# Hybrid decoder layer on one core: the mixing stage's last third in a new order, the exponent's argument split between GpSimd and ScalarE

## The chip, the cores and the metric

One core of a Trainium2 chip. The metric is the device time of one execution in microseconds, median of several runs. Engines: TensorE (PE, its weight loads PEld), VectorE (DVE), ScalarE (ACT), GpSimd (POOL) and SyncE (SP, which here only starts DMA transfers). A queue's name with a q (SPq, ACTq) stands for what that engine issues.

## The reference, cut to what matters

A layer with three groups of heads on one normed input (1024 prompt tokens, 8 sample tokens, width 1024), then an MLP. The part that the change touches is the mLSTM group (4 heads of 96, chunks of 128 tokens) and, in its order, the pooling group:

```python
bcum = jnp.cumsum(lfb, axis=-1)
D = bcum[..., :, None] - bcum[..., None, :] + ib[..., None, :]
D = jnp.where(mask, D, -jnp.inf)
m_t = jnp.maximum(g, jnp.max(D, axis=-1))
S = jnp.einsum('bhtd,bhsd->bhts', qb, kb) * jnp.exp(D - m_t[..., None])
num = jnp.einsum('bhts,bhsd->bhtd', S, vb) + inter[..., None] * jnp.einsum('bhvk,bhtk->bhtv', C, qb)
...
s = cg[:, PBUF+1:PBUF+1+L] - cg[:, PBUF+1-win:PBUF+1-win+L]     # pooling: windows 2, 4, 8, 16
diff = s / cnt[None, :, None] - u
outs.append(jnp.einsum('blc,cd->bld', diff, pool_w[gi]) * pool_scale[gi])
```

## The kernel before, in words

The whole layer runs feature-major in fp32. Each dense product is made of three matmuls for each of 8 row tiles (high part by high, low by high, high by low, lines 2407 to 2409), so 24 matmuls of 344 tokens for one output tile and one of the three token ranges. The high part of a tile or weight is a ScalarE copy into fp32r (lines 1234, 1239), the low part a GpSimd subtraction (w_lo, line 1082; lo, line 1087).

**The order of work** of the mixing stage is written out by hand in MIX_ORDER (lines 92 to 171). Every engine walks the same list and does its own share of each word, in that order, so a word's place sets its place in the queue of each engine. The words of the stretch:

- D:u:c, dense product of unit u and token range c. ScalarE empties its bank (D0, D1, D2). For units 14 to 16 it applies a gelu (line 1331), VectorE multiplies by the LRU result (line 1870), then come the high and low parts, which are pieces of Y.
- W:u, split of the weights of unit u. W_hi has two cells, so ScalarE waits for the last product of unit u-2; GpSimd follows with W_lo. Unit 17 is the first of the output projection, which starts the stage after this one.
- ADA, ADT, ADM: modulation products on TensorE, their turn (line 2392), and the addition on VectorE (line 1717). R:n: ScalarE issues the DMA of raw weights n.
- LD:c: SyncE loads K, Q, V and NM of mLSTM chunk c. NM (minus m_t over the tokens, broadcast to 128 partitions, 256 KB) has one buffer; the load waits on SyncE for the semaphore of the previous chunk (line 884). From chunk 2 on, LD also waits for U:c-2 and B:c-2.
- EX:c: VectorE adds COL's column and NM into EX (line 1885), takes the minimum with MASK (line 1886), and ScalarE takes the exponent in place (line 1368). S:c: TensorE turns K into the bank X3 (line 2498, KT:c) and multiplies K by Q (line 2502, bank X0). SX:c: VectorE scales K into KW (line 1892, frees X3) and multiplies EX by S (line 1895).
- AB:c: Q by state (line 2514, B, bank X2) and EX by V (line 2520, A, bank X1). NU:c: VectorE scales B into T1 (line 1900) and adds A into NUM (line 1903), which frees both banks. HN:c (lines 1907 to 1914, then a square root on ScalarE, line 1371) and HM:c (lines 1918, 1919) norm the result; U:c and CN:c (lines 2528, 1923, 1925) bring the state forward.
- Y:c: TensorE turns the result (line 2536, bank X3); YD:c: VectorE multiplies it by the gate (line 1936, three instructions) and frees X3, then high and low parts; SyncE loads the next gate (load_o).
- POOLV:j, the window sums of pooling tile j: tile 0 on GpSimd, tile 1 on VectorE (lines 1949 to 1953 and ten instructions of lines 1060 to 1065). POOLS copies half of them on ScalarE, POOLD takes the difference (tile 0 on GpSimd, line 1135; tile 1 on VectorE, line 1965). POOL:j:c multiplies by the pooling weights (line 2549) into X1 for c 0 and 2, X2 for c 1; POOLY:j:c reads the bank twice on ScalarE (lines 1392, 1393), and GpSimd makes the low part.

So POOL:0:0 needs X1 from NU:6, and POOL:1:c needs POOLD:1. The X banks are handed out in the order of the list, each use waits for the one before it to be freed (take, line 2362). ScalarE loads another table (ACT_TABLE_LOAD) when it changes between exponent, square root and gelu.

Of the kernel before, what the change touches and what calls it, by code (L numbers as in the profile page):

```python
# [17 lines left out]
ALU = mybir.AluOpType  # L18
# [6 lines left out]
D = 1024  # L25
# [10 lines left out]
HEADS, HD = 4, 96  # L36
# [51 lines left out]
def unit_of(kind, t):  # L88
# [109 lines left out]
def bank_uses(plan):  # L198
# [8 lines left out]
    for s in plan:  # L207
# [7 lines left out]
        elif k == "ADT":  # L215
            add(s, "X1" if s[1] in ADA_START else "X4" if s[1] == NPAIR - 1 else "X3")
# [73 lines left out]
def build(nc, I, O):  # L290
# [24 lines left out]
    with ExitStack() as ctx:  # L315
# [197 lines left out]
        ex_ready, ex_exp, cn_ready = sem("ex_ready"), sem("ex_exp"), sem("cn_ready")  # L513
# [284 lines left out]
        def _(sp):  # L798
# [26 lines left out]
            for s in plan:  # L825
# [41 lines left out]
                elif k == "LD":  # L867
# [15 lines left out]
                    if c >= 1:  # L883
                        sp.wait_ge(ex_ready, c)
# [193 lines left out]
        def _(pool):  # L1078
# [25 lines left out]
            for s in plan:  # L1104
# [108 lines left out]
        def _(act):  # L1213
# [55 lines left out]
            for s in plan:  # L1269
# [407 lines left out]
        def _(dve):  # L1677
# [78 lines left out]
            for s in plan:  # L1756
# [1129 lines left out]
```

## Time and profile before

| | |
|---|---|
| three runs, median | 1175.29 us (1174.09 to 1179.2) |
| the profiled execution | 1175.78 us, span 1174.0 us |
| busy in the span | PE 1124.6 us (96%), DVE 792.8 (68%), ACT 473.4 (40%), POOL 346.9 (30%) |
| granted TensorE clock, mean | 0.982 |
| changed stretch | from about 228 us (first loads of mLSTM chunk 0) to 383.5 us (first output product) |

Busy time is time in which an engine executes something. TensorE's matmuls overlap; its idle time is read from the waits, where each row says which instruction stood still and whose result it waited for. The granted clock is given as a share of 2.4 GHz; 0.5 is 1.2 GHz. The share of one engine in the whole span says little here: the stages differ, and in the MLP, from about 500 us on, TensorE has no idle time at all.

### The profile page before, as it was taken

Reading aid. Unit: us, or ns where it says so; the run is one execution under the profiler, and the core shown is the slowest. Engines: PE = TensorE matmul, PEld = TensorE weight load, DVE = VectorE, ACT = ScalarE, POOL = GpSimd, SP = SyncE. Lnnn points to the kernel's source line nnn. Section 1 sums busy time; section 2 is a strip of 40 time slices with the busy share of each in tenths; the row PEclk is TensorE's granted clock in tenths of the full one; section 3 lists DMA queues with packets and bytes.
Section 4 is the critical chain, followed back from the end, with each engine's and each line's share of the span. In section 5 each row is a group of like instructions: output and inputs, shape, how many; then the busy total and the mean of one; then the engine's idle time right before and its main releaser. Section 6 shows DMA issues by size and latency. Waiting matters only on the chain.

```text
span 1174.0 us, 19681 instructions
## 1 busy us (share of the span) xinstructions
PE 1124.6 (96%) x7237; PEld 1077.3 (92%) x7237; DVE 792.8 (68%) x1319; ACT 473.4 (40%) x780; POOL 346.9 (30%) x275
## 2 busy tenths in 40 slices
PE   4799999999989999999999999999999999999997
PEld 1598888888979999899999999999999999999996
DVE  4561455478775434678578878778778788788546
ACT  5551355655456344642233332332432433433431
POOL 0442011201434357764032022132131231231352
PEclk9699999998989999999999999999999999999998
DMA  8912523566523722111111111202102202111104
GB/s 302 326 57 88 142 90 126 177 180 218 176 87 113 269 90 73 54 55 37 37 36 55 54 37 55 71 18 71 56 16 75 68 18 72 53 50 58 37 1 145
DMA packets 67846, 109.85 MB, mean 94 GB/s; under 512 B 6435, under 2 KB 42567, under 8 KB 67399
## 3 DMA queue, kind: packets, MB, share of 16 engines
q1 hardware_dynamic: 57574, 84.88, 22.0%
q10 hardware_dynamic: 10208, 24.12, 6.6%
q8 instruction: 41, 0.67, 0.2%
q14 instruction: 23, 0.18, 0.0%
HBM read 96.81 MB, written 12.18 MB: 93 GB/s over the span
## 4 chain that ended last, share of the span: by engine, by line
PE 82%; DVE 9%; ACT 3%; DMA 2%; issue 1%; POOL 1%; SPq 1%; ACTq 0%; POOLq 0%; DVEq 0%
PE D L2407 7%; PE D L2409 7%; PE D L2408 7%; PE D L2591 6%; PE D L2593 5%; PE D L2592 5%; PE X L2593 5%; PE X L2591 5%; PE X L2592 5%; PE X L2663 5%; PE X L2664 5%; PE X L2665 5%; PE D L2663 2%; PE D L2665 2%; PE D L2664 2%; DMA RAWW<-in_WADA 2%
## 5 line engine op out<-in xcount | busy, mean ns | idle before, releaser
L2407 PE MATMUL D<-H_hi,W_hi 128*128 128x344 f32 x472 | 158.6, 336 | 3.7 <-POOL H_lo L1087 3.1
L2409 PE MATMUL D<-H_hi,W_lo 128*128 128x344 f32 x472 | 152.4, 323 | 0.0
L2408 PE MATMUL D<-H_lo,W_hi 128*128 128x344 f32 x472 | 152.4, 323 | 0.0
L1087 POOL TENSOR_TENSOR Y_lo<-FU,Y_hi 128x344 fp32r<-128x344 f32 (+3 forms) x84 | 100.1, 1194 | 154.2 <-ACT Y_hi L1521 88.5
L1082 POOL TENSOR_TENSOR W_lo<-RAWW,W_hi 128x1024 fp32r<-128x1024 f32 x25 | 61.6, 2465 | 182.5 <-ACT W_hi L1234 182.2
L1087 POOL TENSOR_TENSOR Y_lo<-EY,Y_hi 128x344 fp32r<-128x344 f32 (+1 forms) x24 | 38.3, 1598 | 216.3 <-ACT Y_hi L1521 144.5
L2407 PEld LDWEIGHTS D<-H_hi,W_hi 128*128 128x128 f32 x472 | 90.5, 192 | 11.8 <-issue 7.6
L2408 PEld LDWEIGHTS D<-H_lo,W_hi 128*128 128x128 f32 x472 | 90.3, 191 | 0.9 <-issue 0.5
L2409 PEld LDWEIGHTS D<-H_hi,W_lo 128*128 128x128 f32 x472 | 90.2, 191 | 0.0
L2215 DVE SCALAR_TENSOR_TENSOR X<-X,MOD 128x344 f32<-128x344 f32 (+1 forms) x138 | 75.7, 566 | 9.2 <-PE X L2665 9.0
L2663 PE MATMUL X<-Y_hi,W_hi 128*128 128x344 f32 x252 | 80.7, 320 | 0.0
L2664 PE MATMUL X<-Y_lo,W_hi 128*128 128x344 f32 x252 | 80.6, 320 | 0.0
L2665 PE MATMUL X<-Y_hi,W_lo 128*128 128x344 f32 x252 | 80.5, 319 | 0.0
L2017 DVE SCALAR_TENSOR_TENSOR X<-D,MOD,X 128x344 f32<-128x344 f32 (+1 forms) x72 | 41.3, 573 | 45.4 <-PE D L2593 24.7
L2407 PE MATMUL D<-Y_hi,W_hi 128*128 128x344 f32 x192 | 62.0, 323 | 1.5 <-POOL W_lo L1082 1.5
L1099 POOL TENSOR_TENSOR SS<-SS,SQ 128x344 f32<-128x344 f32 x45 | 43.3, 963 | 65.9 <-ACT SQ L1430 40.5
L1087 POOL TENSOR_TENSOR Y_lo<-KEPT,Y_hi 128x344 fp32r<-128x344 f32 x24 | 26.4, 1098 | 120.7 <-ACT Y_hi L1521 120.7
L2408 PE MATMUL D<-Y_lo,W_hi 128*128 128x344 f32 x192 | 61.3, 319 | 0.0
L2409 PE MATMUL D<-Y_hi,W_lo 128*128 128x344 f32 x192 | 61.3, 319 | 0.0
L1556 ACT ACTIVATE W_hi<-RAWW 128x1024 fp32r<-128x1024 f32 x30 | 31.8, 1059 | 64.3 <-PE X L2665 55.6
L2378 PE MATMUL X<-RAWW,CTX 128*32 128x256 f32 x384 | 35.7, 461 | 19.5 <-DMA RAWW<-in_WADA 19.4
L1087 POOL TENSOR_TENSOR H_lo<-FU,H_hi 128x344 fp32r<-128x344 f32 (+2 forms) x33 | 29.9, 914 | 66.2 <-ACT FU L1252 50.7
(416 smaller groups left out, 3455.1 us busy)
## 6 DMA issues: line engine op xcount, KB each, us to landing
RAWW<-in_W SPq DMA_DIRECT2D x76, 512.0 KB, 3.6
RAWW<-in_WADA ACTq DMA_DIRECT2D x28, 512.0 KB, 4.1
RAWW<-in_WADA SPq DMA_DIRECT2D x20, 512.0 KB, 8.0
RAWW<-in_W ACTq DMA_DIRECT2D x18, 512.0 KB, 3.7
X0T<-in_x SPq DMA_DIRECT2D x3, 1376.0 KB, 12.8
out_y<-OUTN SPq DMA_DIRECT2D x24, 172.0 KB
X<-in_x SPq DMA_DIRECT2D x8, 344.0 KB, 5.3
NM<-nm_d SPq DMA_DIRECT2D x8, 256.0 KB, 5.3
```

What stands on the lines that cost most here:

```text
L1082: nc.gpsimd.tensor_tensor(lo_v, RAWW[:, raw, :] if src is None else src[:], hi_v.bitcast(F32), ALU.subtract).then_inc(w_lo_ready, 1)
L1087: nc.gpsimd.tensor_tensor(lo_v, fu_v, hi_v.bitcast(F32), ALU.subtract).then_inc(lo_ready, 1)
L2215: V.scalar_tensor_tensor(out=X[:, m, c * CH:c * CH + w], in0=ps[:, 0:w], scalar=MOD[:, 5 * KT + m, 0:1], in1=X[:, m, c * CH:c * CH + w], o ...
L2407: T.matmul(out, w_h, hi[:, kt, a:b], start=(kt == 0), stop=False)
L2408: T.matmul(out, w_h, lo[:, kt, a:b], start=False, stop=False)
L2409: one = T.matmul(out, w_l, hi[:, kt, a:b], start=False, stop=(kt == KT - 1))
L2591: T.matmul(out, w_h, hi(kt), start=(kt == 0 and not onto), stop=False, skip_group_check=onto)
L2592: T.matmul(out, w_h, lo(kt), start=False, stop=False, skip_group_check=onto)
L2593: one = T.matmul(out, w_l, hi(kt), start=False, stop=(kt == n - 1), skip_group_check=onto)
L2663: T.matmul(bank[:, 0:CH], w_hi[:, a:a + P], h, start=(start and k == 0), stop=False, skip_group_check=onto)
L2664: T.matmul(bank[:, 0:CH], w_hi[:, a:a + P], l, start=False, stop=False, skip_group_check=onto)
L2665: one = T.matmul(bank[:, 0:CH], w_lo[:, a:a + P], h, start=False, stop=(stop and k == 1), skip_group_check=onto)
```

## The change

The exponent: GpSimd adds MASK to NM in place (new word NX:c, one instruction of 128x512) as soon as NM has landed. ScalarE takes the exponent straight from NM into EX with COL's column as bias, one instruction per head (four of 128x128) in place of one of 128x512. VectorE's two instructions go, and with the minimum goes the cap of the exponent's argument at 0. ScalarE now waits for A:c-1 before it writes EX. NM is loaded again after the exponent, no longer after VectorE's addition.

The order: NX:c+1 stands after NU:c (NX:6 after ADM:21, NX:7 before EX:7). YD:0 stands ahead of HN:4. W:15 moves behind NU:5 and HN:5; ADM:21 and EX:6 move ahead of HM:5. NU:6, Y:3, POOL:0:0 and POOL:0:1 with their POOLY stand before POOLV:1; HN:6, LD:7 and HM:6 move into D:15:0; R:60 moves to D:14:0; W:17 moves from D:16:1 to D:15:2. ADT:22 writes bank X4 in place of X3.

```diff
--- before.py
+++ after.py
@@ -144,29 +144,28 @@
 D:8:1 R:43
 D:8:2 R:42 ADA:16:1 R:44 W:10 LD:0 SMA TS TSD ADT:16 LRUM:2
 D:9:0
-D:9:1 R:46 R:45 LD:1 ADM:16 EX:0 ADA:17:0 S:0 SX:0 ADA:17:1 W:11 AB:0 R:47
-D:9:2 ADT:17 U:0 NU:0 HN:0 CN:0 ADM:17 HM:0 EX:1 ADA:18:0 SMK S:1 SX:1 SMB:0
+D:9:1 R:46 R:45 LD:1 ADM:16 NX:0 EX:0 ADA:17:0 S:0 SX:0 ADA:17:1 W:11 AB:0 R:47
+D:9:2 ADT:17 U:0 NU:0 NX:1 HN:0 CN:0 ADM:17 HM:0 EX:1 ADA:18:0 SMK S:1 SX:1 SMB:0
 D:10:0 LD:2
-D:10:1 LD:3 AB:1 NU:1 ADA:18:1 U:1 CN:1 HN:1
+D:10:1 LD:3 AB:1 NU:1 NX:2 ADA:18:1 U:1 CN:1 HN:1
 D:10:2 HM:1 R:49 R:48 LD:4 EX:2 W:12
-D:11:0 SMB:1 S:2 SX:2 AB:2 NU:2 ADT:18 U:2 CN:2 ADM:18 HN:2 R:50
+D:11:0 SMB:1 S:2 SX:2 AB:2 NU:2 NX:3 ADT:18 U:2 CN:2 ADM:18 HN:2 R:50
 D:11:1 SMB:2 HM:2 R:52 EX:3 ADA:19:0 S:3 SX:3
-D:11:2 SMB:3 AB:3 ADA:19:1 W:13 LDO:0 R:51 NU:3
+D:11:2 SMB:3 AB:3 ADA:19:1 W:13 LDO:0 R:51 NU:3 NX:4
 D:12:0 ADT:19 U:3 HN:3 HM:3 R:53 CN:3 ADM:19 LD:5 ADA:20:0 EX:4 R:55
-D:12:1 S:4 SX:4 ADA:20:1 Y:0 R:54 SMC AB:4 NU:4
-D:12:2 R:56 U:4 ADT:20 HN:4 W:14 YD:0 R:58 HM:4 LD:6
+D:12:1 S:4 SX:4 ADA:20:1 Y:0 R:54 SMC AB:4 NU:4 NX:5
+D:12:2 R:56 U:4 ADT:20 YD:0 HN:4 W:14 R:58 HM:4 LD:6
 D:13:0 Y:1 ADM:20 CN:4 ADA:21:0 EX:5 YD:1 R:57
-D:13:1 S:5 ADA:21:1 POOLV:0 YS POOLS:0 POOLD:0 SX:5 W:15 YSD AB:5 NU:5 HN:5 HM:5
-D:13:2 ADT:21 R:59 U:5 CN:5
-D:14:0 Y:2 ADM:21 EX:6 YD:2
-D:14:1 ADA:22:0 S:6 SX:6 R:61 AB:6 ADA:22:1 Y:3 POOLV:1
-D:14:2 POOL:0:0 POOLS:1 NU:6 YD:3 R:60 POOLY:0:0 POOL:0:1 ADT:22 POOLY:0:1 HN:6 LD:7 POOL:0:2 POOLD:1 POOLY:0:2 ADM:22
-    HM:6
-D:15:0 U:6 Y:4 POOL:1:0 R:62 CN:6 POOLY:1:0 ADA:23:0 EX:7 POOL:1:1 W:16 R:64 YD:4
+D:13:1 S:5 ADA:21:1 POOLV:0 YS POOLS:0 POOLD:0 SX:5 YSD AB:5 NU:5 HN:5 W:15
+D:13:2 ADT:21 ADM:21 NX:6 EX:6 HM:5 R:59 U:5 CN:5
+D:14:0 R:60 Y:2 YD:2
+D:14:1 ADA:22:0 S:6 SX:6 R:61 AB:6 NU:6 ADA:22:1 Y:3 POOL:0:0 POOLY:0:0 POOL:0:1 POOLY:0:1 POOLV:1
+D:14:2 POOL:0:2 ADT:22 POOLS:1 POOLY:0:2 YD:3 POOLD:1 ADM:22
+D:15:0 HN:6 LD:7 U:6 HM:6 POOL:1:0 Y:4 R:62 CN:6 POOLY:1:0 ADA:23:0 NX:7 EX:7 POOL:1:1 W:16 R:64 YD:4
 D:15:1 POOLY:1:1 S:7 SX:7 POOL:1:2 POOLY:1:2 ADA:23:1 R:63
-D:15:2 Y:5 YD:5 AB:7 NU:7 ADT:23 HN:7
-D:16:0 R:65 HM:7 Y:6 U:7 YD:6 CN:7 ADM:23
-D:16:1 Y:7 W:17 YD:7
+D:15:2 W:17 Y:5 YD:5 AB:7 NU:7 ADT:23 HN:7
+D:16:0 R:65 Y:6 YD:6 HM:7 U:7 CN:7 ADM:23
+D:16:1 Y:7 YD:7
 D:16:2
 """
 
@@ -213,7 +212,7 @@
         elif k == "ADA" and s[2] == 0:
             add(("ADA", s[1]), "X3" if s[1] in ADA_START[::2] else "X4")
         elif k == "ADT":
-            add(s, "X1" if s[1] in ADA_START else "X4" if s[1] == NPAIR - 1 else "X3")
+            add(s, "X1" if s[1] in ADA_START else "X4" if s[1] >= NPAIR - 2 else "X3")
         elif k in ("G1", "G2", "G3", "G4", "Y", "YS"):
             add(s, "X3")
         elif k == "TS":
@@ -510,7 +509,7 @@
         ts_stored, u_diff = sem("ts_stored"), [sem(f"u{j}_diff") for j in range(POOL_T)]
         ld_kqv = [sem(f"ld_kqv{b}") for b in range(2)]
         ld_nm, ld_o, ld_mask = sem("ld_nm"), sem("ld_o"), sem("ld_mask")
-        ex_ready, ex_exp, cn_ready = sem("ex_ready"), sem("ex_exp"), sem("cn_ready")
+        nm_masked, ex_exp, cn_ready = sem("nm_masked"), sem("ex_exp"), sem("cn_ready")
         z_ready, z_root, hm_ready = sem("z_ready"), sem("z_root"), sem("hm_ready")
         sma_t, sma_e, sr_stored = sem("sma_t"), sem("sma_e"), sem("sr_stored")
         ld_st, ld_s, ld_bdl = sem("ld_state"), sem("ld_s"), sem("ld_bdl")
@@ -881,7 +880,7 @@
                         sp.dma_start(dst[:], src.rearrange("(h d) t -> d h t", d=HD)[:, :, c * LC:(c + 1) * LC]).then_inc(ld_kqv[b], 16)
                     sp.dma_start(VB[b][:].rearrange("p h v -> p (h v)"), v_d[c]).then_inc(ld_kqv[b], 16)
                     if c >= 1:
-                        sp.wait_ge(ex_ready, c)
+                        sp.wait_ge(ex_exp, c)
                     sp.dma_start(NM[:], nm_d.rearrange("(h c) t -> c h t", c=NLC + 1)[c].partition_broadcast(P)).then_inc(ld_nm, 16)
                 elif k == "SMA":
                     sp.wait_ge(sma_e, 2)
@@ -1121,6 +1120,11 @@
                 elif k == "POOLY":
                     key = ("POOL", *s[1:])
                     lo(full_at[key], *views(key))
+                elif k == "NX":
+                    if s[1] == 0:
+                        pool.wait_ge(ld_mask, 16)
+                    pool.wait_ge(ld_nm, 16 * (s[1] + 1))
+                    nc.gpsimd.tensor_tensor(NM[:], NM[:], over(MASK[:], HEADS), ALU.add).then_inc(nm_masked, 1)
                 elif s == ("POOLV", 0):
 
                     pool.wait_ge(h_ready, LRU_T)
@@ -1364,8 +1368,16 @@
                     act.wait_ge(gv, 4)
                     nc.scalar.activation(GR[:, R_EM, :], GR[:, R_EM, :], ACT.Exp, scale=-1.0).then_inc(ga, 1)
                 elif k == "EX":
-                    act.wait_ge(ex_ready, s[1] + 1)
-                    nc.scalar.activation(EX[:], EX[:], ACT.Exp).then_inc(ex_exp, 1)
+                    c = s[1]
+                    if c == 0:
+                        b, n = use[("G4",)]
+                        act.wait_ge(x_free[b], n + 1)
+                    else:
+                        wait_full(act, ("A", c - 1))
+                    act.wait_ge(nm_masked, c + 1)
+                    for h in range(HEADS):
+                        one = nc.scalar.activation(EX[:, h, :], NM[:, h, :], ACT.Exp, bias=colh(0, c)[:, h:h + 1])
+                    one.then_inc(ex_exp, 1)
                 elif k == "HN":
                     act.wait_ge(z_ready, s[1] + 1)
                     nc.scalar.activation(SM4[:, 5, :], SM4[:, 4, :], ACT.Sqrt, bias=EPT[:], scale=1.0 / HD).then_inc(z_root, 1)
@@ -1874,16 +1886,9 @@
                         wait_full(dve, ("TS", w))
                         put_free(V.tensor_copy(QK8[:, w, :], bank(("TS", w))[0:DEC, 0:HEADS * HD]), ("TS", w))
                 elif k == "EX":
-                    c = s[1]
-                    if c == 0:
+                    if s[1] == 0:
                         tell(V.memset(CN[:], 0.0), cn_ready, 1)
                         dve.wait_ge(ld_dec, 16)
-                        dve.wait_ge(ld_mask, 16)
-                    else:
-                        wait_full(dve, ("A", c - 1))
-                    dve.wait_ge(ld_nm, 16 * (c + 1))
-                    link(V.tensor_tensor(EX[:], NM[:], wide(colh(0, c), LC), ALU.add))
-                    tell(V.tensor_tensor(EX[:], EX[:], over(MASK[:], HEADS), ALU.min), ex_ready, c + 1)
                 elif k == "SX":
                     c = s[1]
                     if c:
```

## Rows read from the trace of the kernel before

**Rows 1.** The profile page, first line.

```profile
span 1174.0 us, 19681 instructions
```

**Rows 2.** Busy by stretch: length, PE, PEld, DVE, ACT, POOL (instructions), clock, DMA, GB/s.

```profile
700.00:800.00 100.00, 100.00 (x637) 100.00 (x636) 81.83 (x132) 35.24 (x54) 23.78 (x17) 1.00 0.15 48
```

**Rows 3.** Waits from 225 to 400 us: in total, times, longest.

```profile
PE X L2549 <- DVE NUM L1903: 3.7, 1, 3.7
...
PE X L2520 <- DVE EX L1895: 2.9, 3, 1.7
...
PE D L2407 <- POOL W_lo L1082: 1.5, 1, 1.5
...
PE X L2536 <- DVE MOD L1717: 1.5, 1, 1.5
...
PE X L2392 <- DVEq L1941: 0.9, 1, 0.9
```

**Rows 4.** Busy by stretch, columns as in rows 2.

```profile
230.00:240.00 10.00, 8.99 (x73) 7.67 (x72) 6.80 (x18) 2.64 (x4) 0.00 (x0) 1.00 0.86 256
266.00:278.00 12.00, 10.33 (x59) 9.55 (x58) 9.48 (x19) 5.29 (x7) 2.34 (x1) 0.72 0.59 199
344.00:354.00 10.00, 9.24 (x40) 7.85 (x41) 7.57 (x15) 7.38 (x12) 5.20 (x5) 0.68 0.61 158
```

**Rows 5.** The tile EX: count, ns min/median/max, first and last start.

```profile
L1886 DVE TENSOR_TENSOR EX<-EX,MASK x8: 691/693/1302, 234.0 to 356.9; 128x512 f32<-128x512 f32 x8
L1368 ACT ACTIVATE EX<-EX x8: 629/632/635, 235.3 to 358.3; 128x512 f32<-128x512 f32 x8
```

**Rows 6.** Line 1363, a ScalarE instruction with a bias from memory.

```profile
L1363 ACT ACTIVATE GR<-GR x1: 387/387/387, 134.7 to 134.7; 36x128 f32<-36x128 f32 x1
```

**Rows 7.** ScalarE in order of time: start us, duration us.

```profile
346.37 0.55 ACT L1392 ACTIVATE Y_hi<-X,COLS 128x344 fp32r<-128x344 f32 x1
346.81 0.54 ACT L1393 ACTIVATE FU<-X,COLS 128x344 f32<-128x344 f32 x1
...
358.27 0.64 ACT L1368 ACTIVATE EX<-EX 128x512 f32<-128x512 f32 x1 [0.51 <-DVE EX L1886]
...
358.81 1.04 ACT L1234 ACTIVATE W_hi<-RAWW 128x1024 fp32r<-128x1024 f32 x1
...
360.28 1.28 ACT L1331 ACT_TABLE_LOAD   x1
```

**Rows 8.** GpSimd by line and form, 310 to 385 us: busy us, mean ns.

```profile
L1087 POOL TENSOR_TENSOR Y_lo<-FU,Y_hi 128x344 fp32r<-128x344 f32 x15 | 14.9, 995 | 26.5 <-ACT Y_hi L1239 25.0 <-ACT FU L1393 1.4
...
L1082 POOL TENSOR_TENSOR W_lo<-RAWW,W_hi 128x1024 fp32r<-128x1024 f32 x3 | 7.1, 2376 | 2.3 <-ACT W_hi L1234 2.2
```

**Rows 9.** The tile NM, time of its eight loads.

```profile
DMA to landing us min/median/max: 3.2/5.3/7.2
```

**Rows 10.** GpSimd in order of time.

```profile
286.67 2.40 POOL L1082 TENSOR_TENSOR W_lo<-RAWW,W_hi 128x1024 fp32r<-128x1024 f32 x1 [18.02 <-ACT W_hi L1234]
```

**Rows 11.** VectorE in order of time.

```profile
286.86 2.62 DVE L1912 TENSOR_TENSOR HM<-NUM,SM 128x384 f32<-128x384 f32 x1
...
335.05 0.19 DVE L1949 COPY UO<-ST 128x15 f32<-128x15 f32 x1
...
344.65 1.12 DVE L1936 SCALAR_TENSOR_TENSOR FU<-X,COLS,OT 128x128 f32<-128x128 f32 x3
...
349.63 1.29 DVE L1965 SCALAR_TENSOR_TENSOR ST<-PB,COLS,ST 128x1024 f32<-128x1024 f32 x1
...
362.88 0.56 DVE L1892 TENSOR_TENSOR KW<-X,COL 128x384 f32<-128x384 f32 x1 [0.21 <-DVEq L1969]
```

**Rows 12.** TensorE in order of time.

```profile
366.62 0.49 PE L2536 MATMUL X<-IDN,HM 128*128 128x128 f32 x3
...
367.82 0.39 PE L2520 MATMUL X<-VB,EX 128*128 128x97 f32 x2
```

**Rows 13.** SyncE's DMA queue in order of time.

```profile
347.78 0.43 SPq L885 DMA_DIRECT2D NM<-nm_d  x1
```

## The prediction, made before the change was run

> **What bounds the kernel now.** Read first how busy TensorE is. The profiled execution took 1175.8 us around a span of 1174.0 [rows 1]. In the MLP TensorE is busy all the time, 637 matmuls in 100 us, 0.157 us each, so 3.8 us for a dense product of 24 [rows 2]. Whatever reaches that phase earlier ends earlier. So the question is what TensorE loses in the changed stretch. The waits name it [rows 3]: 3.7 us for NUM, 2.9 for EX (three times, longest 1.7; the other two are 1.0 and 0.2), 1.5 for MOD, 1.5 for W_lo, 0.9 for the queue of VectorE. The granted clock adds to it [rows 4]: from 266 to 278 us it is 0.72 of full speed, from 344 to 354 us 0.68, where TensorE worked at 1.2 instead of 2.4 GHz for a time. Both dips begin with an idle TensorE among small products, 1.7 and 3.7 us of it; the stretch of 230 to 240 us, small products with a wait of 1.0 us, kept 1.00. The dips cost 12 x 0.28 = 3.4 us and 10 x 0.32 = 3.2, of which 0.4 is idle time counted already: 2.8.
>
> **The change part by part.** Waits first, then what is new.
>
> *Exponent off VectorE.* VectorE loses two instructions of 0.69 us a chunk [rows 5], with their links 1.45 us, eight times. It gets nothing in return. Where it leads TensorE this is a gain at once. EX:2 does so: VectorE's product of EX ends 1.45 us earlier if ScalarE's exponent is ready. ScalarE now has four instructions of 128x128 with a bias from memory. The nearest row is 0.387 us for 36x128 with a bias [rows 6]; two neighbours of 0.55 start 0.44 apart [rows 7], so four take 3 x 0.29 + 0.39 = 1.3 us (1.2 to 1.6) where one took 0.63 [rows 5]. The exponent of EX:2 waits there for ScalarE's own earlier work and ends 0.7 later than before, so of 1.7 us of wait about 0.6 stays: 1.1 gained (0 to 1.7). With that wait below the 1.0 us that did no harm, the first slow clock should go: 3.4.
>
> *NX on GpSimd.* 128x512 lies between 1.0 us for 344 columns and 2.4 for 1024 [rows 8]: by a straight line 1.3 (1.0 to 2.4). It reads and writes NM in place, before its chunk is due. At chunk 0 nothing hides it: NM lands, then 1.3 + 1.3 where 2 x 0.72 + 0.63 stood, and the wait of 1.0 us grows by some 0.1 net of hops (0 to 0.6). Cover for chunks 1 to 5: NM is loaded one to three dense products before the exponent is wanted. The reload now starts after the exponent instead of after the addition, some 2 us later in the chunk's course, plus 5.3 us to land (3.2 to 7.2) [rows 9]: 5.3 + 1.3 + 1.3 = 8 us against a chunk every (356.9 - 234.0) / 7 = 17.6 us [rows 5]. That costs nothing except at chunk 7.
>
> A row speaks against GpSimd as the place: a VectorE instruction of 0.56 us took 2.62, starting 0.2 us after a GpSimd subtraction of 2.40 [rows 10, 11]. NX overlaps VectorE in most chunks. Yet the mask instruction's worst case is 1.30 against a median of 0.69 [rows 5], 0.6 us more, and VectorE is then mostly waiting anyway. I cost the seven later NX at nothing on the path (bound: 1.3 each).
>
> *Order at the first of the Y turns.* YD:0 now precedes HN:4 on VectorE, some 2.4 us earlier; ADT:20 waited 0.9 us for its bank [rows 3]. Gone: 0.9 (0 to 0.9).
>
> *ADM:21 and HN:5's root.* Y:2 waits 1.5 us for MOD [rows 3], because ADM:21 stood behind HM:5 and CN:5, and HM:5 behind a square root that ScalarE could take only after W:15, which waits for D:13:2. ADM:21 comes first now and the root goes ahead of W:15: 1.5 gained (1.0 to 1.5).
>
> *EX:6 earlier on ScalarE.* What it adds is a queue. From the end of D:13:2: W_hi 1.0 [rows 7], W_lo 2.4 [rows 8], NX 1.3, exponent 1.3, a table load 1.3 [rows 7], the gelu of D:14:0 0.5, its VectorE product 0.5, YD:2 1.1 [rows 11], two high parts on ScalarE 1.0, the next gelu and its product 1.0, KW 0.6, EX 0.7: 12.7 us. TensorE in that time: two dense products 7.6, four small groups of 0.5, three of eight matmuls at 0.9 [rows 12]: 12.3. So A:6 waits about 0.4 and the hops: 0.8 for 0.2 before, 0.6 lost (0 to 2).
>
> *NU:6 ahead of the pooling sums.* This is the large one. POOL:0:0 needs the bank that NU:6 frees, and NU:6 stood behind the sums on VectorE, which began at 335.05 [rows 11]. Now it is read right after A:6, and the 3.7 us go, and with them the slow clock, 2.8. What is late next is POOL:1:0, which needs POOLD:1. VectorE from the end of A:6: NUM 0.6, sums and the gelu product 344.65 - 335.05 - 2 x 0.6 = 8.4, YD:3 1.1, POOLD:1 1.3 [rows 11]: 11.4. TensorE: two dense 7.6, six small groups 3.0, U:6 0.9 [rows 12]: 11.5. Even, with hops 0.1 late. But the two GpSimd low parts of POOLY:0:0 and 0:1 now run beside the sums, which ran alone. By the row of 1.30 against 0.69 each costs VectorE 0.6: a wait of 1.3 (0 to 2.5). The Trainium skill (SBUF - State Buffer, "Who interferes with whom") states that a VectorE instruction with two SBUF inputs and a reading GpSimd one exclude each other for the whole instruction. By that rule and 1.0 us a low part the wait would be 2.1 and the total 0.8 us later.
>
> *ADT:22 in bank X4.* It no longer waits for YD:3, and ADA:23 waits for ADM:22, which VectorE does before TensorE comes: 0 (0 to 0.5).
>
> *Chunk 7.* LD:7 is printed elsewhere, but on SyncE's queue it still stands behind YD:3's load. YD:3 starts at about 340.2 instead of 344.65 [rows 11]: A:6 starts at 335.05, when EX is ready, less the 6.2 us gained so far, runs 1.1 [rows 12], then 0.6 + 8.4 + 1.2. So NM is issued at 343.4 instead of 347.8 [rows 13], lands 5.3 later, NX 1.3, exponent 1.3: 351.3, where it ended at 358.9 [rows 7]. KW:7 ended at 363.4 [rows 11], now 355.8. TensorE is at Y:5, which needs KW's bank, at 366.6 [rows 12] less 11.4, 355.2: 0.7 lost with hops (0 to 2.5).
>
> *W:17 early.* TensorE waits 1.5 us for W_lo [rows 3], which GpSimd makes last of all. It is made a dense product and more sooner: 1.5 gained (1.0 to 1.5). R:60 and W:15 are moved on ScalarE past a product's copy only; their loads are covered by two dense products: 0.
>
> Sum: 1.1 + 3.4 + 0.9 + 1.5 + 3.7 + 2.8 + 1.5 = 14.9 gained; 0.1 + 0.6 + 1.3 + 0.7 = 2.7 lost; net 12.2. From 1175.8 that is 1163.6. The execution profiled is 0.5 above the median of 1175.3, so the forecast is 1163.1.
>
> **The rivals.** (a) *GpSimd's turn rules the exponents.* NX waits behind a W_lo or is shut out by VectorE, and ScalarE stands at EX with gelus behind it. For it: the row of 2.62. At EX:6 and EX:7, which have no slack by the sums above, NX at 2.4 and one blocked low part more cost some 2 us each: 1167. Against: six of eight chunks have slack. (b) *The slow clock stays or moves.* The new waits at A:6 and Y:5 lie among small products, as the old ones did; a dip like those costs 3.4: 1166.5 with one, 1169.5 with both. Against: none of the new waits is over 1.3 us in my sum. (c) *The change does not do what it says:* NU:6 must wait for A:6, the sums start later, and the wait goes whole from POOL:0:0 to POOL:1:0, 3.7 us with its clock of 2.8 where I have 1.3: 1168.3. Speaks for it: VectorE and TensorE are even over 11.4 us. (d) *Slower.* NM has one buffer and its reload starts after the exponent. If load, NX and exponent took longer than a chunk, every chunk would wait. At 7.2 + 2.4 + 1.6 = 11.2 us the point of 17.6 is not reached; but where SyncE stands at LD:c for the exponent, the loads behind it start late too. At 2.4 us for each of the eight chunks, a W_lo's length [rows 8], 19.2 us on top, the time is 1182.3. It decides if the exponent comes over one dense product late in every chunk.
>
> **How the numbers follow.** Forecast 0.55, (a) 0.14, (b) 0.13, (c) 0.12, (d) 0.06. A measurement tells about 0.5%, 5.9 us: faster is under 1169.4, slower over 1181.2. All of the first, most of (a) and (b) and two thirds of (c) are faster: 0.80. The rest, 0.14, stays within 0.5%; slower 0.06. The low end takes every gain and no new wait: 1175.3 - 14.9 = 1160.4, 1159.5 with VectorE quicker elsewhere. The high end takes both slow clocks or (c) with a late chunk 7: 1171.
>
> **What would show it.** TensorE's wait for NUM gone and a short one for the pooling difference or EX instead; W_lo's and MOD's waits gone; granted clock 1.00 from 230 to 350 us; NX near 1.3 us and four exponents of 0.39. The first output product should start about 12 us sooner. I am wrong if a wait over 2 us stands at POOL:1:0, Y:5 or A:6, or if the clock still dips.

## The result: 6.5 us slower, where 12 us faster was forecast

| | before | after |
|---|---|---|
| median (lowest to highest) | 1175.94 us (1174.09 to 1179.2), 7 runs | 1182.43 us (1181.07 to 1182.95), 7 runs |
| ratio | 1 | 1.0059 (95%: 1.0044 to 1.0073) |
| execution profiled | 1175.78 us, span 1174.0 | 1181.23 us, span 1179.4 |
| start of the first output product | 383.55 us | 389.21 us |

The ratio and its interval are worked out from all runs of both kernels, so it need not equal the quotient of the medians.

The first view is again that of TensorE's waits in the stretch of the change (engine, line, who was waited for: us in total, times, longest), of the changed kernel; [rows 3] is its counterpart. Its line numbers lie 5 higher on TensorE than before (L2503 is L2498 there).

```profile
PE X L2503 <- DVEq L1946: 5.8, 2, 3.3
PE X L2541 <- DVE HM L1924: 3.3, 1, 3.3
PE X L2525 <- DVE EX L1900: 3.1, 2, 2.6
PE X L2503 <- DVE MOD L1729: 0.8, 2, 0.5
PE X L2541 <- DVE KW L1897: 0.6, 1, 0.6
PE D L2412 <- DVE W_lo L2039: 0.2, 1, 0.2
```

Four of the five waits that the change aimed at are gone: NUM (3.7 us), MOD at Y:2 (1.5), W_lo (1.5, a rest of 0.2), VectorE's queue at ADT:20 (0.9). In their place stand three that the prediction did not have: KT:6 and KT:7 wait for the bank X3 (L2503, 3.3 and 2.5 us), and Y:7 waits for HM:7 (3.3). AB:0 waits 2.6 us for EX where it waited 1.0. Of the signs of being wrong that the prediction named, the clock's dips came; waits over 2 us came as well, but not at POOL:1:0, Y:5 or A:6, where it looked for them.

The clock, by stretches (columns as in [rows 4]), of the changed kernel:

```profile
235.00:245.00 10.00, 7.40 (x30) 7.40 (x31) 4.55 (x10) 2.02 (x6) 0.00 (x0) 0.66 0.80 212
325.00:335.00 10.00, 6.65 (x45) 5.99 (x44) 3.03 (x6) 6.06 (x11) 3.28 (x4) 0.89 0.35 119
335.00:345.00 10.00, 10.00 (x47) 8.07 (x47) 6.92 (x15) 2.44 (x6) 3.07 (x3) 0.59 0.20 59
385.00:395.00 10.00, 9.85 (x56) 9.57 (x55) 4.38 (x9) 4.05 (x7) 4.26 (x5) 0.88 0.71 224
```

The dip at 266 us of [rows 4] is gone, but one of the same size begins at 238 us; the one at 344 us now lies at 330 to 345 us and is larger; a third comes at 385. They follow the longer waits at AB:0, KT:6 and Y:7; the 2.5 us at KT:7 brought none in this execution. Read 335:345 with care: PE is "busy" for all 10.00 us, yet with 47 matmuls instead of some 64 at [rows 2]'s rate. That is a clock of 1.2 GHz for most of the stretch (0.59 on average), not work.

### The profile page after: what moved, and what is told of

Its sections match the earlier page's. It is cut to its first block, busy times and chain, and to the rows that moved or that the text cites. A ratio compares the mean times of both kernels' runs of the same rounds, so it can differ in the third digit from the quotient of the medians.

```text
span 1179.4 us, 19693 instructions
## 1 busy us (share of the span) xinstructions
PE 1128.3 (96%) x7237; PEld 1080.5 (92%) x7237; DVE 786.4 (67%) x1303; ACT 475.9 (40%) x802; POOL 357.3 (30%) x283
## 4 chain that ended last, share of the span: by engine, by line
PE 76%; DVE 10%; ACT 5%; DMA 3%; POOL 2%; issue 2%; SPq 1%; ACTq 0%; DVEq 0%; POOLq 0%
PE D L2412 6%; PE D L2596 6%; PE D L2598 5%; PE D L2597 5%; PE D L2414 5%; PE D L2413 5%; PE X L2598 5%; PE X L2596 5%; PE X L2597 5%; PE X L2668 5%; PE X L2670 5%; PE X L2669 5%; PE D L2668 2%; PE D L2670 2%; PE D L2669 2%
## 6 DMA issues: line engine op xcount, KB each, us to landing
X0T<-in_x SPq DMA_DIRECT2D x3, 1376.0 KB, 12.6
```

## An account of the stretch

One sum puts all kernels of this study side by side (what each is, the next section tells): TensorE's waits from 225 to 405 us, plus what the clock cost there, 10 us x (1 - granted clock) over its 18 stretches of 10 us.

| kernel | ratio to before (95%) | waits | clock | sum | span - sum |
|---|---|---|---|---|---|
| before | 1 | 11.4 | 6.8 | 18.2 | 1155.8 |
| after | 1.0059 (1.0044 to 1.0073) | 13.8 | 10.3 | 24.1 | 1155.3 |
| e1_swap | 1.0010 (0.9991 to 1.0030) | 14.0 | 3.4 | 17.4 | 1157.0 |
| e2_order_only | 1.0015 (0.9993 to 1.0037) | 14.1 | 5.1 | 19.2 | 1155.7 |
| e3_exp_only | 1.0041 (1.0020 to 1.0061) | 14.7 | 8.6 | 23.3 | 1154.4 |
| e4_exp_only_swap | 1.0008 (0.9985 to 1.0031) | 12.4 | 5.1 | 17.5 | 1156.7 |
| e5_yd4 | 1.0034 (1.0020 to 1.0049) | 12.6 | 6.8 | 19.4 | 1155.7 |
| e6_ex6 | 1.0018 (1.0003 to 1.0033) | 12.9 | 8.5 | 21.4 | 1156.1 |
| e7_hm7 | 1.0015 (0.9998 to 1.0032) | 14.2 | 5.1 | 19.3 | 1156.1 |
| e8_all | 1.0026 (1.0014 to 1.0039) | 13.0 | 10.2 | 23.2 | 1155.5 |
| e9_nu6 | 1.0019 (1.0008 to 1.0030) | 12.2 | 6.8 | 19.0 | 1155.8 |
| e10_heads | 1.0015 (0.9999 to 1.0030) | 11.4 | 12.0 | 23.4 | 1153.3 |
| e11_w17 | 0.9997 (0.9982 to 1.0013) | 12.9 | 1.7 | 14.6 | 1155.3 |
| e12_nm0_before | 0.9984 (0.9968 to 1.0000) | 11.7 | 5.1 | 16.8 | 1156.6 |
| e13_nm0_after | 1.0055 (1.0038 to 1.0072) | 13.2 | 6.8 | 20.0 | 1155.0 |
| e14_nm0_swap | 1.0025 (1.0011 to 1.0039) | 15.1 | 6.8 | 21.9 | 1155.1 |
| e15_best | 1.0029 (1.0015 to 1.0044) | 13.7 | 8.5 | 22.2 | 1155.9 |
| e16_nm0_w17 | 1.0011 (0.9998 to 1.0023) | 12.7 | 5.1 | 17.8 | 1155.1 |
| e17_mix | 1.0012 (0.9998 to 1.0026) | 13.4 | 3.4 | 16.8 | 1155.3 |
| e18_r45 | 1.0005 (0.9991 to 1.0019) | 11.1 | 6.8 | 17.9 | 1155.2 |

The last column is the span of the execution profiled less the sum: 1155.5 us on average, within 1.5 of it everywhere but once (e10_heads, 2.2). So, to within that, nothing is lost outside this stretch, and nothing given back later: the forecast's 12 us vanished between 225 and 405 us, by waits and clock. The ratios rest on all runs of a kernel, the sums on one execution each, and that one can lie far from the median: e13_nm0_after was profiled in its fastest run (1176.85 us, median 1180.96), e17_mix in its fastest too (1173.88, median 1176.53), e11_w17 3.1 us below its median. Compare kernels by the ratio, and use the sums only to see where the time of one execution went.

## The experiments

**The table load behind the late wait.** The changed kernel has two waits ahead of ScalarE's exponent, for A:c-1 (G4's bank at chunk 0) and for the masked NM. In the traces the last of the two in the program holds up the ACT_TABLE_LOAD that is put ahead of the ACTIVATE, and the first holds up the ACTIVATE itself. ScalarE around AB:0, in order of time (start us, duration us, what ended the idle time before); first the changed kernel:

```profile
232.03 0.90 ACTq L555 DMA_DIRECT2D RAWW<-in_WADA  x2
234.19 1.28 ACT L1379 ACT_TABLE_LOAD   x1 [2.30 <-POOL NM L1127]
235.49 1.28 ACT L1379 ACTIVATE EX<-NM,COL 128x128 f32<-128x128 f32 x4
```

then the kernel before:

```profile
232.75 1.18 ACTq L556 DMA_DIRECT2D RAWW<-in_WADA  x2
233.96 1.28 ACT L1368 ACT_TABLE_LOAD   x1 [1.35 <-issue]
235.25 0.63 ACT L1368 ACTIVATE EX<-EX 128x512 f32<-128x512 f32 x1
```

Before, the table load ran as soon as ScalarE had issued its two loads, beside VectorE's addition and minimum. After, ScalarE stood idle for 2.30 us until GpSimd's NX was done, and only then loaded the table. The same row at chunk 6 of the changed kernel, where ScalarE stands longest; ScalarE, then VectorE, then TensorE:

```profile
326.45 1.28 ACT L1379 ACT_TABLE_LOAD   x1 [3.96 <-POOL NM L1127]
327.75 0.40 ACT L1379 ACTIVATE EX<-NM,COL 128x128 f32<-128x128 f32 x1
...
329.05 1.28 ACT L1335 ACT_TABLE_LOAD   x1
330.35 0.46 ACT L1335 ACTIVATE GT<-D 128x344 f32<-128x344 f32 x1
```

```profile
330.89 0.52 DVE L1882 TENSOR_TENSOR FU<-GT,HS 128x344 f32<-128x344 f32 x1 [7.42 <-ACT GT L1335]
331.44 1.12 DVE L1941 SCALAR_TENSOR_TENSOR FU<-X,COLS,OT 128x128 f32<-128x128 f32 x3
```

```profile
332.77 0.80 PE L2503 MATMUL X<-IDN,K 96*128 96x96 f32 x4 [3.35 <-DVEq L1946]
```

ScalarE waits 3.96 us for NX:6, loads the exponent's table, takes the exponent, loads the gelu's table, and only then comes the gelu of D:14:0, for which VectorE had stood 7.42 us. YD:2 follows it and frees X3, for which KT:6 waits. e1_swap exchanges the two waits:

```diff
-                    if c == 0:
-                        b, n = use[("G4",)]
-                        act.wait_ge(x_free[b], n + 1)
-                    else:
-                        wait_full(act, ("A", c - 1))
                     act.wait_ge(nm_masked, c + 1)
+                    if c == 0:
+                        b, n = use[("G4",)]
+                        act.wait_ge(x_free[b], n + 1)
+                    else:
+                        wait_full(act, ("A", c - 1))
```

> The changed kernel with ScalarE's two waits ahead of the exponent exchanged, so that the wait for GpSimd's mask addition sits on the first exponent and no longer on the table load ahead of it. Theory T (the table load of 1.28 us has come onto the path of every exponent whose NX is late, chunks 0, 6 and 7): the load runs during the wait, the wait at AB:0 falls from 2.6 to about 1.3 us and its slow clock goes (10 x 0.14 + 10 x 0.21 = 3.5 us), KT:6 waits 2.1 instead of 3.35: 1182.4 - 1.3 - 3.5 - 1.3 = about 1176, and less if the second slow clock goes too. Theory O (the new order is at fault, the exponent is not): at most 1.3 us better, 1181.

Measured 1.0010 of before against 1.0059: 1176.73 us, 5.7 less. Chunk 6 of e1_swap on ScalarE:

```profile
322.08 1.28 ACT L1379 ACT_TABLE_LOAD   x1
325.98 0.41 ACT L1379 ACTIVATE EX<-NM,COL 128x128 f32<-128x128 f32 x1 [2.62 <-POOL NM L1127]
```

The load ran 2.6 us ahead of the operand. That one exchange, which moves no work, takes back nearly the whole loss. It did not do it as expected: AB:0 still waits 2.2 us, not 1.3 (NM landed later in this execution), and the waits sum to 14.0 us where the changed kernel has 13.8. What fell is the clock's cost, from 10.3 to 3.4 us. Most of that is at chunk 6: KT:6 waits 2.0 us instead of 3.35, and behind it the clock stays at 1.00 (columns as in [rows 4]), where the changed kernel had 0.89 and 0.59 (5.2 us):

```profile
325.00:335.00 10.00, 7.13 (x57) 6.30 (x56) 4.44 (x8) 4.87 (x10) 3.76 (x4) 1.00 0.51 142
335.00:345.00 10.00, 10.00 (x67) 8.90 (x67) 8.62 (x17) 2.81 (x6) 3.59 (x2) 1.00 0.10 36
```

The same pair in the old order, e3_exp_only (new exponent, MIX_ORDER of before with an NX word behind each NU, and NX:0 and NX:7 ahead of their EX) and e4_exp_only_swap (the same, waits exchanged), and the new order with the old exponent, e2_order_only. The diff, cut, is that of e3_exp_only against before, MIX_ORDER alone:

```diff
-D:9:1 R:46 R:45 LD:1 ADM:16 EX:0 ADA:17:0 ...
+D:9:1 R:46 R:45 LD:1 ADM:16 NX:0 EX:0 ADA:17:0 ...
...
-D:13:1 ... AB:5 NU:5 HN:5 HM:5
+D:13:1 ... AB:5 NU:5 NX:6 HN:5 HM:5
```

> New order and the X4 bank for ADT:22, exponent as before the change (addition and minimum on VectorE, one ScalarE instruction, NM reloaded after the addition). Theory T and its wider form E (the exponent on GpSimd and ScalarE is what costs): the order alone gives the gains forecast for it, waits for NUM, MOD and W_lo gone, about 1176 - 6 = 1170. Theory O: as slow as the whole change or slower, 1180 to 1185, with the waits at KT:7 and Y:7 still there.

> Old order and bank, exponent as in the change (NX behind NU of the chunk before; NX:6 behind NU:5, NX:7 ahead of EX:7). Theory E: slower than before, the wait at AB:0 2.6 us with a slow clock at 240 us as in the changed kernel: 1176 + 1.6 + 3.5 = 1181 or more. Theory O: 1176 or faster, as VectorE has 11.6 us less to do.

> The old order with the new exponent and the two waits exchanged. Theory T: the table load was the loss, so this is no slower than before the change: 1172 to 1176, wait at AB:0 about 1.3 us, clock 1.00 at 240 us. If only GpSimd's place in the chain costs (NX behind W_lo, one NM buffer), it stays near the run without the exchange, within 2 us.

Exponent alone 1.0041, with the exchange 1.0008: 3.3 thousandths, some 4 us, in the old order too, though their intervals overlap a little. And the parts themselves: new order with the old exponent 1.0015, new exponent with the exchange 1.0008, both together (e1_swap) 1.0010. Neither part gains what the sum gave it. e2_order_only came out between its two theories (1170 and 1180 or more): the waits for NUM and MOD are gone, but without any new exponent KT:7 waits 4.3 us for X3, and 1.8 us stand at POOL:1:0, 1.7 for KW and 1.6 for HM:7. The rest of the study asks where the gain went.

**Single waits of the new order.** The largest that e1_swap still has (waits, columns as above):

```profile
PE X L2503 <- DVEq L1946: 4.5, 2, 2.5
PE X L2525 <- DVE EX L1900: 3.8, 3, 2.2
PE X L2554 <- DVE ST L1970: 1.8, 1, 1.8
PE X L2541 <- DVE HM L1924: 1.8, 1, 1.8
PE D L2412 <- DVE W_lo L2039: 1.3, 1, 1.3
```

Three runs take away the cause of one each, on top of e1_swap, and e8_all does all three: e5_yd4 puts YD:4 ahead of HN:6 (it frees X3 for KT:7), e6_ex6 puts EX:6 behind YD:2, e7_hm7 puts HM:7 ahead of YD:6.

```diff
-D:15:0 HN:6 LD:7 U:6 HM:6 POOL:1:0 Y:4 R:62 ... W:16 R:64 YD:4
+D:15:0 LD:7 U:6 Y:4 YD:4 HN:6 HM:6 POOL:1:0 R:62 ... W:16 R:64
...
-D:13:2 ADT:21 ADM:21 NX:6 EX:6 HM:5 ...
+D:13:2 ADT:21 ADM:21 NX:6 HM:5 ...
-D:14:0 R:60 Y:2 YD:2
+D:14:0 R:60 Y:2 YD:2 EX:6
...
-D:16:0 R:65 Y:6 YD:6 HM:7 U:7 ...
+D:16:0 R:65 Y:6 HM:7 YD:6 U:7 ...
```

> From the version with the two waits exchanged (e1, 1176.7 us): in D:15:0 LD:7 first, then U:6, Y:4 and YD:4 ahead of HN:6, HM:6 and CN:6. Theory Q (the remaining loss is what the new order queues in front of X3's release: YD:4 now stands behind HN:6, HM:6 and CN:6, where before the change it stood behind HM:6 and CN:6 alone with HN:6 long done): TensorE's wait at KT:7, 2.5 us, goes, about 1.5 of it to be kept: 1175. Rival: the wait at KT:7 only moves to Y:5 or AB:7, as EX:7 sets both: time unchanged at 1176 to 1177.

> From e1: EX:6 behind the gelu of D:14:0 and YD:2 on ScalarE, its place before the change, all else new. Theory Q: ScalarE no longer stands 2.6 us for NX:6 with the gelu of D:14:0 behind it, VectorE's YD:2 frees X3 in time, the wait at KT:6 (2.0 us) goes and the one at A:6 (0.9) stays or grows by up to 1: 1175. Rival: VectorE is what is late there, and the wait comes back whole at A:6 or POOL:1:0: 1176 to 1177.

> From e1: HM:7 ahead of YD:6, as before the change. Theory Q: the wait at Y:7, 1.8 us, falls by YD:6's 1.1 us on VectorE to 0.7 or less: 1175.5. Rival: that wait is set by HN:7's root on ScalarE and nothing changes, and the 1.3 us for a low weight part in the next stage stays too.

> From e1: the edits of e5, e6 and e7 together. If the waits at KT:6, KT:7 and Y:7 (6.3 us in all) are each caused by what is queued in front and not by VectorE's whole load, they go together and the time is 1170 to 1172, faster than before the change by 0.3% to 0.5%. If VectorE as a whole sets the pace from 330 us on, the waits turn up at POOL:1:0 and A:7 and the time is 1174 to 1176.

None of the four brought its gain: 1.0034, 1.0018, 1.0015 and 1.0026, none better than e1_swap, and all but e7_hm7 slower than before beyond their intervals. Their waits tell why. e5_yd4 (the rows that are new):

```profile
PE X L2541 <- DVE HM L1924: 3.3, 1, 3.3
...
PE X L2507 <- DVE CN L1930: 1.8, 1, 1.8
```

KT:7 no longer waits, but S:7 right behind it waits 1.8 us for CN:6, which now stands behind YD:4, and Y:7's wait grew from 1.8 to 3.3. e6_ex6:

```profile
PE X L2525 <- DVE EX L1900: 6.2, 3, 3.1
```

KT:6 no longer waits, but A:6 does, 3.06 us at 333.64. So EX:6 is early for the one and late for the other. e7_hm7:

```profile
PE X L2541 <- DVEq L1946: 3.3, 1, 3.3
```

Y:7 no longer waits for HM:7 but for YD:6, which frees its bank and now stands behind HM:7. In each case TensorE needs two results of VectorE within a few us, and whichever goes first, it waits for the other. In e8_all the waits at KT:6 and KT:7 and for HM:7 are all gone, and in their place stand 6.1 us for EX (3.1 of them at A:6), 3.0 for KW at two places and 1.8 for CN:6. What was removed as a wait was a place in a queue. VectorE was busy for 7.58 and 8.67 us of the two stretches of 10 us from 330 to 350 in e1_swap.

**Single parts of the order on the kernel before.** e9_nu6 takes the large term alone (NU:6 and the first pooling products ahead of POOLV:1, HN:6 to HM:6 behind, R:60 earlier, ADT:22 in X4), e10_heads takes YD:0, ADM:21 and HN:5, e11_w17 takes W:17. The diff is that of e11_w17:

```diff
-D:15:2 Y:5 YD:5 AB:7 NU:7 ADT:23 HN:7
+D:15:2 W:17 Y:5 YD:5 AB:7 NU:7 ADT:23 HN:7
...
-D:16:1 Y:7 W:17 YD:7
+D:16:1 Y:7 YD:7
```

> The kernel before with one part of the new order alone: NU:6 and the pooling products of the first group ahead of the pooling sums (POOLV:1), R:60 earlier, HN:6, LD:7 and HM:6 after the sums, ADT:22 in bank X4; exponent, W:15, ADM:21 and W:17 as before. If the prediction's largest term stands by itself, the wait of 3.7 us for NUM and the slow clock of 2.8 behind it go and a wait of 1.3 comes: 5.2 us less than before, about 1170.7 us. Rival: the stretch from 300 to 390 us is bound by VectorE's queue, so the wait turns up again at KT:7 (for YD:4), at POOL:1:0 or at Y:7, 4 us and more together: within 1.5 us of before, and the waits and the slow clock of 225 to 405 us add up to 17 to 19 us as before (18.2).

> The kernel before with YD:0 ahead of HN:4, the root of HN:5 ahead of W:15, and ADM:21 ahead of HM:5 and CN:5; the rest as before. If these terms of the prediction stand by themselves, the waits of 0.9 us at ADT:20 and 1.5 us for MOD at Y:2 go: 2.4 us less, about 1173.5 us. Rival: the wait for NUM at POOL:0:0 grows by what TensorE comes earlier, 2.4 us: 1175.9 us as before, with NUM at 6 us.

> The kernel before with W:17 printed before Y:5 instead of after Y:7. If the term stands by itself, TensorE's wait of 1.5 us for W_lo at the first output product goes and nothing comes: about 1174.4 us. Rival: the low half of W:17 on GpSimd, 2.4 us, now runs beside the short VectorE instructions of HN:7 and stretches them, as it does in the changed kernel (1.47 and 0.93 us instead of 0.17 each): HM:7 comes 2 us later, Y:7 waits for it, and the time is 1175.5 to 1177 us.

e9_nu6 came to 1.0019, some 2 us over before and beyond its interval. The rival's mechanism holds, and the cost is a little over what it allowed (1.5 us). Its new waits:

```profile
PE X L2497 <- DVEq L1940: 2.7, 1, 2.7
PE X L2548 <- DVE ST L1964: 1.8, 1, 1.8
```

The 3.7 us for NUM are gone, and 2.7 at KT:7 and 1.8 at POOL:1:0 have come; the clock cost 6.8 us as before. e10_heads: 1.0015; MOD's wait went and NUM fell from 3.7 to 2.4, but 1.7 us for KW came and the clock cost 12.0 in the execution profiled. e11_w17: 0.9997, so neither the gain of 1.5 us nor the rival's loss is shown: W_lo's 1.5 us became 1.4 for VectorE's W_lo and 1.7 for YD's bank at a Y turn.

**Chunk 0.** With NM's first load issued before SyncE's wait for the stores of k, q and v, the operand is there early. e12_nm0_before does it to the kernel before, e13_nm0_after to the changed one, e14_nm0_swap to e1_swap, e15_best to e4_exp_only_swap with W:17 early. The diff is cut:

```diff
                     if c == 0:
+                        sp.wait_ge(nm_stored, 16)
+                        sp.dma_start(MASK[:], I["mask"]).then_inc(ld_mask, 16)
+                        sp.dma_start(NM[:], nm_d...[0]...).then_inc(ld_nm, 16)
                         for i in range(2):
                             sp.wait_ge(st_stored[i], 16 * st_count(LAST_KQ + 1, i))
```

> The kernel before, with the mask and the first load of NM issued in LD:0 ahead of SyncE's wait for the stores of k, q and v (they start 4 us sooner, and need none of these stores). TensorE's wait at AB:0 (1.0 us in the execution profiled, 0.9 to 1.3 in others of the same code) goes. The slow clock there is seen in few executions of the old exponent, so little more: 1.0 to 1.5 us less than before, 1173.2 to 1173.8 us where before is 1174.6. Rival: what TensorE gains at AB:0 comes back as a longer wait at EX:2 and POOL:0:0: no difference, with EX and NUM 1 us longer together.

> The changed kernel with the mask and the first load of NM issued in LD:0 ahead of SyncE's wait for the stores. NX:0, the table load and the four exponents of chunk 0 then lie beside TensorE's small products: the wait of 2.6 us at AB:0 goes, and the slow clock of 3.4 us behind it. If chunk 0 is the place where the changed kernel loses most against the forecast, it takes 6 us less: 1176.4 us. The table loads at EX:6 and EX:7 stay. Rival: the gain is given back from 300 us on, at KT:6, KT:7 and Y:7, as in the other runs, and it stays over 1180 us.

> The changed kernel with the two waits of ScalarE exchanged and the first load of NM early. Against the exchange alone (1176.7 us) the wait of 2.2 us at AB:0 and its slow clock of 1.7 us go: 1172.8 us. Rival: given back at KT:6 and KT:7, which wait for VectorE's queue: 1176.7 us.

> Old order, new exponent with its two waits exchanged, W:17 printed before Y:5, first load of NM early. From the exchange in the old order (1176.8 us): the wait of 1.9 us at AB:0 and its slow clock of 1.7 go, W_lo's 1.5 us are half given back: 1172.5 us, under the kernel before by 2 us, if single gains in the first chunk reach the end. Rival: they are given back at POOL:0:0, which waits for NUM (3.7 us there): 1176 us, with NUM over 6 us.

0.9984, 1.0055, 1.0025 and 1.0029: only the first is below 1, its interval ends at 1, and its median is only 0.3 us below. The wait at AB:0 did not go, because NM was not the only late thing. ScalarE of e13_nm0_after:

```profile
230.68 0.90 ACTq L555 DMA_DIRECT2D RAWW<-in_WADA  x2
231.66 1.28 ACT L1380 ACT_TABLE_LOAD   x1 [1.12 <-issue]
232.96 1.28 ACT L1380 ACTIVATE EX<-NM,COL 128x128 f32<-128x128 f32 x4
```

With NM there, ScalarE's own queue sets the end: a copy, the issues of R:46 and R:45, the table, the exponents. In e14_nm0_swap the table load stands on the other wait, which is now the later one ("1.43 <-DVE KW"), and starts at 232.54. The last three follow that up: e17_mix is the changed kernel with the early load and the order of the two waits chosen by chunk (masked NM last at chunk 0, first at the others), e16_nm0_w17 is e12_nm0_before with W:17 early, and e18_r45 prints R:46 and R:45 behind EX:0 on top (its diff is the one shown).

```diff
-D:9:1 R:46 R:45 LD:1 ADM:16 EX:0 ADA:17:0 ...
+D:9:1 LD:1 ADM:16 EX:0 R:46 R:45 ADA:17:0 ...
```

> The kernel before with the first load of NM early and W:17 printed before Y:5. Singly these measured 0.9984 and 0.9997 of the kernel before. If they add: 0.998, some 2 us less. Rival: no more than the early load alone, and the interval holds 1.

> The changed kernel with the first load of NM early and, on ScalarE, the wait for the masked NM last at chunk 0 (as in the changed kernel) and first at chunks 1 to 7 (exchanged). The table load then stands on the wait that comes first in every chunk. Chunk 0 as in the run with the early load alone (wait at AB:0 1.4 us, no slow clock in the execution profiled), chunks 6 and 7 as in the run with the exchange: 1175 us where before is 1174.1, waits and slow clock 16 to 18 us together. Rival: as for the exchange with the early load, 1.0025 of before, 1177 us.

> As the run with the early load of NM and W:17 early on the kernel before, and R:46 and R:45, two loads of weights that ScalarE issues (1.10 us), printed after EX:0 instead of before it. With NM early the chain at AB:0 is ScalarE's: its copy, these two issues, the table load of 1.28, the exponent of 0.63. Without the issues ahead the table load starts 1.1 to 1.3 us sooner and TensorE's wait of 0.9 us at AB:0 goes: 1 us less than that run. Rival: the next waits (EX:2, NUM) take it back: no difference to that run.

e17_mix: 1.0012, as e1_swap; chunk 0 adds nothing that the ratios show. Against e13_nm0_after (1.0055) it differs in the order of the two waits at chunks 1 to 7 alone. It is thus a third pair for the table load, with intervals that do not touch, and places most of the cost: KT:6 waits 2.0 us instead of 3.3, and the clock of 325 to 345 us is 1.00 instead of 0.60 and 0.89 (5.1 us). e18_r45 took the wait at AB:0 away altogether. ScalarE of it:

```profile
231.44 1.28 ACT L1369 ACT_TABLE_LOAD   x1
...
232.73 0.63 ACT L1369 ACTIVATE EX<-EX 128x512 f32<-128x512 f32 x1
```

AB:0's product then began at 234.36, without a wait; still 1.0005, and e16_nm0_w17 1.0011. That e12_nm0_before (0.9984) is a gain is therefore not shown: with more waits removed, the ratio is 1 again. No version of the study beats the kernel before beyond its interval.

## Why the prediction was wrong, by its own steps

The sum had 8.7 us of waits gone, 2.7 come and 6.2 us of clock given back. In the executions profiled the waits rose from 11.4 to 13.8 us and the clock's cost from 6.8 to 10.3: a miss of 8.4 us in waits and 9.7 in clock. The steps that failed:

**"At chunk 0 nothing hides it ... grows by some 0.1."** It grew by 1.6, to 2.6 us. The arithmetic of the work was right: NX took 1.255 to 1.289 us (1.3 forecast), four exponents 1.28 (1.3). In e1_swap the chain from NM's landing to AB:0's product measured 3.41 us (234.91 to 238.32), before it measured 3.43. Left out was the table load of 1.28 us: a row with its price stood in [rows 7], and I took for granted that it runs ahead of the wait as before, where only one wait was there. The Trainium skill (ScalarE: Activation LUTs, "Step-by-step: what each stage is for") says that the compiler places the table load "right before this ACTIVATE". The trace agrees, and it shows what that means with two waits: the load takes over the last of them. Exchanging the waits gave back 5.7 us, but e17_mix got it back with chunk 0 left as it was: the cost lies at the later chunks, most of it in the clock behind KT:6, and chunk 0's share shows in no ratio.

**"EX:6 earlier on ScalarE ... A:6 waits about 0.4."** I counted the chain (12.7 us) and set it against TensorE's way to A:6. It leads to YD:2, and YD:2 frees X3 for KT:6, which TensorE reaches first. KT:6 waited 3.3 us, A:6 not at all. The chain itself was longer by the table load, by NX:6's place on GpSimd (behind a W_lo of 2.78 us, done at 325.12), and ScalarE stood idle for it. The forecast put nothing here for the clock; 5.2 us came with this wait. This is rival (a)'s mechanism, at one chunk.

**"LD:7 is printed elsewhere"**: the step looked at NM alone. HN:6 and HM:6 went past D:14:2's end, close in front of YD:4 on VectorE, and KT:7 needs the bank that YD:4 frees: 2.5 us, shown again in e2_order_only (4.3) and e9_nu6 (2.7) without the new exponent. An instruction that moves counts for all that stands behind it.

**"W:17 early: 1.5 gained."** The wait went to 0.2, but W_lo now runs beside HN:7. VectorE of the changed kernel, then GpSimd:

```profile
374.26 1.47 DVE L1912 SCALAR_TENSOR_TENSOR SM<-NUM 128x4 f32<-128x4 f32 x1
375.76 0.93 DVE L1913 TENSOR_TENSOR SM<-SM,COL 128x4 f32<-128x4 f32 x1
376.72 0.18 DVE L1914 RECIPROCAL SM<-SM 128x4 f32<-128x4 f32 x1
```

```profile
373.31 2.39 POOL L1081 TENSOR_TENSOR W_lo<-RAWW,W_hi 128x1024 fp32r<-128x1024 f32 x1
375.66 1.00 POOL L1086 TENSOR_TENSOR Y_lo<-FU,Y_hi 128x384 fp32r<-128x384 f32 x1
```

Two instructions of 0.17 us each end with GpSimd's (375.73 and 376.69 against 375.70 and 376.66) and so last 2.4 us. By [rows 10, 11] I had that price and applied it only to the low parts beside the sums. The rule named in the prediction (the Trainium skill, SBUF - State Buffer, "Who interferes with whom") is that the second of the two stands for the whole of the first; these ends agree with it, better than my 0.6 us an instruction. With HM:7 behind YD:6 as well, Y:7 waited 3.3 us.

**"With that wait below 1.0 us ... the first slow clock should go."** It went: in the twelve kernels with the new exponent EX:2 waits 0.51 to 1.17 us, and the clock of 265 to 275 us is 1.00 in all of them. In the eight with the old one EX:2 waits 0.59 to 2.07 us and the clock is 0.66 to 0.83 in six, 1.00 in two. But the 3.4 us were booked as a gain with nothing set against them, and in eleven of the twelve the clock of 235 to 245 us is now 0.66 to 0.83, behind AB:0's longer wait (the one without is e13_nm0_after). NUM's slow clock, 2.8, went with the wait for NUM, and a larger one came behind KT:6. Rival (b), that the clock moves, had this at 0.13.

**Right were** NUM's 3.7, MOD's 1.5, ADT:20's 0.9, the first slow clock at its own place, and EX:2's rest (0.5 against 0.6). Y:5's 0.6 against 0.7 is luck: YD:3 began at 349.61 us and not at 340.2, so NM:7 was loaded 9.3 us later than forecast, and TensorE came some 12 us later too. POOL:1:0 with 1.3 shows as 1.8 in e1_swap; in the changed kernel TensorE came too late to wait. Rival (d) named 1182.3 us and 1182.43 was measured, but that too is luck: its condition, an exponent late by a dense product in every chunk, was not met: the exponents of chunks 0, 6 and 7 were late. The forecast's flaw as a whole is in its form: it took waits away one at a time and added what each edit brings to one consumer. With the table load out of the way (e1_swap) the waits still add up to 14.0 us where before had 11.4. What stays open is whether the bound from 300 to 390 us is one resource; that VectorE's order decides each wait there is shown by e5_yd4 to e8_all and e9_nu6, that no order does better is not.

## What to carry to other kernels

Where ScalarE changes tables, put the wait that is ready last first in the program and the early one next to the activation, and look in the trace whether ACT_TABLE_LOAD's idle time names a late operand: here a load of 1.28 us behind a late wait cost 5.7 us, most of it, in the executions profiled, by the slow clock behind the longer wait. When a wait is taken away by moving a word, list for every engine what now stands behind it and who takes its bank next, before the gain is booked; a wait between two engines that are both near their limit moves, it does not go. And test the parts alone: three parts of the order, forecast to gain 5.2, 2.4 and 1.5 us, came to 1.0019, 1.0015 and 0.9997 of before, and the whole order to 1.0015.

## What the runs showed of the hardware beyond that

TensorE's group at AB:0 (eight matmuls, L2520 of before) took 1.13 us at 2.4 GHz and about 2.0 at 1.2. By kernel, the wait ahead of it against its length, twenty executions of the same small products before it:

| wait ahead of AB:0, us | length of the group, us |
|---|---|
| 0 (one), 0.91 to 1.02 (five), 1.32, 1.42 | 1.06 to 1.13: clock at 2.4 GHz |
| 1.33, 1.52, 1.61, 1.73, 1.78, 1.81, 1.90, 1.93, 2.23, 2.60, 2.67, 2.92 | 1.87 to 2.02: clock at 1.2 GHz |

At 1.3 to 1.4 us of wait both levels occur. Where it was the lower one, the clock of 235 to 245 us was 0.83 or 0.66, which is 1.7 or 3.4 us. The table holds for AB:0 alone: after 2.0 us of wait at KT:6 the clock of e1_swap stayed at 1.00. The wait itself hangs on chance as well: NM's first load took 4.5 us to land in the profile of before and 5.6 in that of e1_swap. That may be one reason why executions of one kernel lie up to 8 us apart (1172.17 to 1180.62 us in 29 runs of the kernel before); it is not shown, as only one of the 29 is profiled.

A GpSimd instruction is held up the other way round too: with NM early, NX:0 began at 227.12 us inside VectorE's scan and took 2.38 us instead of 1.27 (e13_nm0_after).
